# Post norms of a decoder layer: weights and squares taken by channel at copy-out, sums of squares on GpSimd and TensorE

## The reference

```python
def rmsnorm(x, g):
    return x * rsqrt(mean(x * x, axis=-1, keepdims=True) + 1e-6) * g

x = x + rmsnorm(merged @ w_out, g_mix_post)                    # token mixing: SSM branch + sparse attention branch
c = rmsnorm(x, g_x_pre)
x = x + rmsnorm(cross_attention(c, mem_kv, w_xq, w_xo), g_x_post)
m = rmsnorm(x, g_mlp_pre)
hid = square(relu(m @ w_up))
x = x + rmsnorm(hid @ w_down, g_mlp_post)
```

## Time and profile before

| | |
|---|---|
| median of three runs | 1191.24 us |
| profiled execution, span | 1194.3 us (no other time of it is recorded) |
| TensorE matmul busy | 1136.4 us, 95% |
| VectorE busy | 635.8 us, 53% |
| ScalarE busy | 461.8 us, 39% |
| GpSimd busy | 166.1 us, 14% |
| mean granted clock of TensorE | 0.987 |
| share of TensorE in the chain that ended last | 77% |

### The profile page before, as it was taken

The page is one execution under the profiler, slowest core; times in us unless marked ns, Lnnn a source line. Parts: engine busy times, 40 slices in busy tenths (PEclk is TensorE's granted clock), DMA queues, the critical chain, the costliest instruction groups (busy, mean ns, idle before and its releaser), DMA issues.

```text
span 1194.3 us, 21756 instructions
## 1 busy us (share of the span) xinstructions
PE 1136.4 (95%) x8378; PEld 1011.1 (85%) x8378; DVE 635.8 (53%) x1143; ACT 461.8 (39%) x755; POOL 166.1 (14%) x281
## 2 busy tenths in 40 slices
PE   6999999999999998999999988999999999999997
PEld 5888787778777676788897987899999989999997
DVE  4467992765665524311537566546543345666663
ACT  3100320455775414200234475454332334545540
POOL 1020024735302222000000020001000000001100
PEclk9999999998999999999999999999999999999998
DMA  7792254734719448454565626742443223232201
GB/s 199 167 230 63 81 181 141 189 108 123 175 51 291 142 142 283 129 166 128 151 190 182 209 72 195 251 141 85 142 142 106 71 76 101 72 106 71 71 1 75
DMA packets 167105, 164.21 MB, mean 137 GB/s; under 512 B 41573, under 2 KB 148034, under 8 KB 166874
## 3 DMA queue, kind: packets, MB, share of 16 engines
q1 hardware_dynamic: 157658, 134.84, 37.7%
q0 software_dynamic: 9344, 27.98, 7.9%
HBM read 154.21 MB, written 12.73 MB: 140 GB/s over the span
## 4 chain that ended last, share of the span: by engine, by line
PE 77%; SPq 7%; DVE 5%; issue 4%; ACT 4%; DMA 1%; POOL 1%; DVEq 0%; ACTq 0%
PE banks L1485 22%; PE banks L1004 15%; PE banks L1740 15%; PE banks L1439 4%; PE banks L1222 3%; SPq L667 2%; PE banks L1421 2%; SPq L647 2%; PE banks L1010 2%; SPq L696 1%; PE banks L1334 1%; DVE rounded L2818 1%; PE banks L1274 1%; PE banks L1285 1%; PE banks L1257 1%
## 5 line engine op out<-in xcount | busy, mean ns | idle before, releaser
L1485 PE MATMUL banks<-rounded 128*128 128x288 f32 (+1 forms) x2304 | 297.4, 289 | 1.4 <-DVE rounded L2864 0.9
L1485 PEld LDWEIGHTS banks<-rounded 128*128 128x128 f32 x2304 | 292.0, 189 | 4.8 <-issue 2.9
L1004 PE MATMUL banks<-arena 128*128 128x256 f32 x960 | 223.9, 393 | 2.3 <-issue 1.8
L1004 PEld LDWEIGHTS banks<-arena 128*128 128x128 f32 x960 | 181.0, 190 | 38.8 <-issue 1.9
L1740 PE MATMUL banks<-rounded 128*128 128x272 f32 x1536 | 195.1, 290 | 3.8 <-DVE rounded L3046 3.8
L1740 PEld LDWEIGHTS banks<-rounded 128*128 128x128 f32 x1536 | 194.5, 190 | 4.5 <-issue 3.1
L2818 DVE TENSOR_TENSOR rounded<-arena,rounded 128x2048 fp32r<-128x2048 f32 x54 | 125.5, 2324 | 65.5 <-ACT rounded L1963 65.4
L3046 DVE TENSOR_TENSOR rounded<-arena,rounded 128x1088 fp32r<-128x1088 f32 x64 | 82.9, 1304 | 60.2 <-ACT rounded L2207 60.2
L1963 ACT ACTIVATE rounded<-arena 128x2048 fp32r<-128x2048 f32 x54 | 102.9, 1906 | 4.1 <-DMA arena<-in_w_out 4.1
L2207 ACT ACTIVATE rounded<-arena 128x1088 fp32r<-128x1088 f32 x64 | 71.1, 1114 | 81.0 <-PE banks L1740 79.8
L2048 ACT ACTIVATE arena<-banks 128x256 f32<-128x256 f32 (+1 forms) x64 | 25.4, 397 | 126.4 <-PE banks L1485 126.4
(11 more groups left out here) (432 smaller groups left out, 1416.5 us busy)
## 6 DMA issues: line engine op xcount, KB each, us to landing
arena<-in_w_up SPq DMA_DIRECT2D x22, 1024.0 KB, 5.6
arena<-in_w_down SPq DMA_DIRECT2D x16, 1024.0 KB, 5.1
arena<-in_w_in SPq DMA_DIRECT2D x13, 1024.0 KB, 8.8
upper<-in_cache_nsa_kv SPq DMA_DIRECT2D x64, 128.0 KB, 2.4
upper<-in_cache_nsa_kv POOLq DMA_DIRECT2D x64, 128.0 KB, 4.7
arena<-in_w_out SPq DMA_DIRECT2D x8, 1024.0 KB, 5.6
arena<-in_cache_mem_kv SPq DMA_DIRECT2D x16, 512.0 KB, 8.1
arena<-in_cache_nsa_kv SPq DMA_DIRECT2D x90, 64.0 KB, 2.3
```

What stands on the lines that cost most here:

```text
L1004: ins = mm(bank(b + h, (NA, NB)[h], rows=M), lhsT(k), rhs[:, k, toks], start=(k == 0), stop=(k == K - 1))
L1485: ins = mm(bank(b, N), w[:, k], a[:, k, toks], start=(k == 0 and z == 0), stop=(k == K - 1 and z == 2))
```

## The change

The squares and the gain of the first two post norms move ahead of the transposes, where the data lie by channel.

- `y_take` now does two ScalarE passes over each unit's bank: a square into `nsq` (two slots in turn), and the copy into `yTA` or `yTB`, with the channel's gain as scale. The gains are loaded by channel into `gnorm` (16 columns) in place of the two rows `gP` and `gP2`.
- GpSimd adds the squares up over the eight units (`square_sums`, six additions for each half and layer into `nsum`; the last square stays separate). ScalarE's square m, from the third on, waits until GpSimd has done sum m-1; the first two wait for the scaling of the half before.
- TensorE multiplies `nsum` and the last square by a column of ones, token tile by token tile (`norm_sums`, matmuls of one column, four for half A and six for half B), which gives the sums by token. They take a turn of the two banks (`("NS", q)` in `late`).
- VectorE scales these (`sums_scale`), GpSimd raises them to -1/2, two token tiles in one call (and one more call for the sample tile in half B).
- `post` is one VectorE pass: transposed tile times root plus x. `y_square` is gone.
- The order of all engines in this part is written anew.

The core of the diff:

```diff
-            sp.dma_start(gP[:, :], A["g_mix_post"][0].partition_broadcast(P)).then_inc(sem("gP_in"), 16)
+            for i, n in enumerate(("g_mix_post", "g_x_post")):
+                sp.dma_start(gnorm[:, i * 8:i * 8 + 8], A[n][0].rearrange("(k p) -> p k", p=P),
+                             allow_slow_non_contiguous=True).then_inc(sem("gP_in"), 16)
...
+            def square_sums(q, first=1, last=7):
+
+                for m in range(first, last):
+                    u = q * 8 + m
+                    w = half_of("AB"[q % 2])[1]
+                    pool.wait_ge(sem("norm_squares"), u + 1)
+                    if m > 1:
+                        pool.wait_ge(sem("norm_sums"), q * 6 + m - 1)
+                    pool.tensor_tensor(nsum[:, 0:w], nsq[:, 0, 0:w] if m == 1 else nsum[:, 0:w], nsq[:, m % 2, 0:w], ALU.add)\
+                        .then_inc(sem("norm_sums"), 1)
...
+            def norm_sums(q):
+
+                b = late_bank(("NS", q), sem("sums_scaled"), q + 1)
+                pe.wait_ge(*step("ones_set"))
+                pe.wait_ge(sem("norm_sums"), q * 6 + 6)
+                pe.wait_ge(sem("norm_squares"), q * 8 + 8)
+                for i, t in enumerate(HALVES[q]):
+                    n, at = tile_rows(t), tok0(t) - tok0(HALVES[q][0])
+                    for j, part in enumerate((nsum, nsq[:, 1])):
+                        ins = mm(bank(b, 1, i, rows=n), part[:, at:at + n], ones, start=(j == 0), stop=(j == 1))
+                signal(ins, "late_mm")
...
                 act.wait_ge(sem("late_mm"), late_at[name] + 1)
-                signal(fn((yTA if half == "A" else yTB)[:, m, :], bank(late_at[name] % 2, N), ACT.Copy), "proj_out")
+                if m >= 2:
+                    act.wait_ge(sem("norm_sums"), q * 6 + m - 1)
+                elif q:
+                    act.wait_ge(sem("sums_scaled"), q)
+                signal(fn(nsq[:, m % 2, 0:N], bank(late_at[name] % 2, N), ACT.Square), "norm_squares")
+                if q == 0 and m == 0:
+                    act.wait_ge(sem("gP_in"), 32)
+                signal(fn((yTA if half == "A" else yTB)[:, m, :], bank(late_at[name] % 2, N), ACT.Copy,
+                          scale=gnorm[:, i * 8 + m:i * 8 + m + 1]), "proj_out")
...
-                link(stt(ps, ps, r, (gP, gP2)[i][0:n, :], ALU.mult, ALU.mult))
-                signal(tt(x[0:n, t, :], x[0:n, t, :], ps, ALU.add), "x_new")
+                dve.wait_ge(sem("post_T"), NT * i + TILES.index(t) + 1)
+                signal(stt(x[0:n, t, :], ps, r, x[0:n, t, :], ALU.mult, ALU.add), "x_new")
```

More of the change, by code:

```diff
@@ L946, in _, with inverse_rms @@
                 sel_pages(pool, gg, 3, known)
-            def inverse_rms(n):
-                for _ in range(n):
-                    e = rms_n[0]
-                    rms_n[0] += 1
-                    n_rows = TS if squares[e][1] == 4 else P
+            def inverse_rms(first, last):
+                for at in range(first, last):
+                    kind, t = roots[at]
+                    if kind == "NS":
+                        pool.wait_ge(sem("sums_scaled"), t + 1)
+                        parts = sum_columns(t)
+                        for n, c, w in parts:
+                            ins = pool.tensor_tensor(rstd2[0:n, c:c + w], var2[0:n, c:c + w], mhalf[0:n].to_broadcast([n, w]), ALU.pow)
+                            ins.then_inc(sem("inverse_rms"), 1)
+                        continue
+                    e = square_at[kind, t]
+                    n_rows = TS if t == 4 else P
                     pool.wait_ge(sem("squares"), e + 1)
@@ L970, in _, with root @@
             signal(pool.memset(qz, 0.0), "qz_zeroed")
-            inverse_rms(20)
+            def root(kind, t):
+                inverse_rms(root_at[kind, t], root_at[kind, t] + 1)
+            square_sums(0)
+            root("NS", 0)
+            root("x0", 0)
+            root("x0", 1)
+            square_sums(1)
+            root("NS", 1)
+            square_sums(2, 1, 2)
+            root("x0", 4)
+            square_sums(2, 2, 3)
+            root("x0", 2)
+            square_sums(2, 3, 5)
+            root("x0", 3)
+            square_sums(2, 5, 7)
+            root("NS", 2)
+            root("x1", 0)
+            root("x1", 1)
+            square_sums(3)
+            inverse_rms(root_at["NS", 3], len(roots))
             for m in range(3):
-                pool.wait_ge(sem("squares"), SQ0 + 4 * m + 4)
+                pool.wait_ge(sem("squares"), SQN + 4 * m + 4)
                 for j in range(2):
@@ L2767, in inverse_rms, with sums_scale @@
             def inverse_rms(kind, t):
-                e = square_at[(kind, t)]
-                dve.wait_ge(sem("inverse_rms"), e + 1)
-                return rstd2[0:P if kind == "mem" else tile_rows(t), e:e + 1]
+                if kind[0] == "y":
+                    q = 2 * int(kind[1]) + (t >= 2)
+                    e, at = y_col[kind, t], roots_done["NS", q]
+                else:
+                    e, at = square_at[kind, t], roots_done[kind, t]
+                dve.wait_ge(sem("inverse_rms"), at)
+                return rstd2[0:P if kind == "mem" else tile_rows(t), e:e + 1]
+            def sums_scale(q):
+                v = late_at["NS", q]
+                dve.wait_ge(sem("late_mm"), v + 1)
+                for n, c, w in sum_columns(q):
+                    ins = ts(var2[0:n, c:c + w], bank(v % 2, w, 0 if n == P else 2, rows=n), 1.0 / D, EPS, ALU.mult, ALU.add)
+                    if q % 2 and n == P:
+                        own(ins)
+                signal(ins, "sums_scaled")
             for t in range(2):
@@ L3011, in _ @@
             hid_square(8)
+            sums_scale(3)
             post(1, 4)
```

143 lines of the change are left out of this document (72 added, 71 removed).

## The result

The changed kernel takes 1196.86 us (median of 15 runs, 1192.87 to 1199.63), the kernel before 1191.24 us in the runs beside it. The ratio, estimated from all runs of the two, is 1.0034, 95% interval 1.0022 to 1.0046: slower by 4.1 us (the two medians are 5.6 us apart). That is inside what I had called no change (0.5%), but on the other side from the forecast of 1189.5 us, and the median lies just above the range. The profiled execution took 1198.49 us, with a span of 1196.5 us against 1194.3 us.

A forecast was written before the change was run, and what follows sets the result against it. TensorE, busy 1136.4 of 1194.3 us, was taken as the bound, with about 12 us to win. Terms 0.1 + 0 + 2.2 + 0 - 0.7 gave 1.6 to 1.7 us: 1191.24 - 1.7 = 1189.5 us, range 1183.8 to 1196.5.

The forecast's parts named there:

- the clock term: B half's query projection was to start at full clock, gaining 0.7 us; no half clock was costed behind the new waits.
- the wait before xoA1: New 2.7 us TensorE wait before the A half's second cross-projection unit, since ScalarE's first take awaits the scaled sums.
- Rival (d): Clock falls again at the query projection and the new wait: 0.7 us not gained, 0.7 lost, 1190.9 us; chance 0.12.
- the first wait: TensorE waits 3.1 us before the A half's second pre transpose; its low part stands behind a split and two passes.
- 615 to 646: Trace stretch in us up to the A half's query projection; early norm given back at a wait, gain 0.1 us.
- 646 to 692: Trace stretch in us with the output projection; square, sum and copy fit even behind a split, change 0.
- 692 to 722: Trace stretch in us up to the B half's query projection: 1.5 us earlier start plus 0.7 of clock, together 2.2.
- 782 to 830: Trace stretch in us with the B half's last cross-projection units: late take and sums outweigh gains, net loss 0.7 us.
- the loop: ScalarE's square and GpSimd's sum wait on each other; 1.2 us a turn, 1.3 for 288 columns, barely fitting the cross projection.
- (c): The removed pass was hidden anyway and the one-column products, 3.5 us, are simply added: 1194.7 us; chance 0.16.
- (b): Slower: the ScalarE-GpSimd loop sets the cross projection's pace, costing 7.5 us: 1197 us; chance 0.15.
- (a): The chains really get shorter: waits and loop holdups do not form, 7.8 us gained, 1183.4 us; chance 0.19.

## Why the prediction was wrong

**What failed** is the clock term. The prediction let the wait before xoA1 form, put the clock behind it at 1.00 and even counted 0.7 us of clock gained at the query projection; the argument was that the new idle pieces are shorter than the old one. The gain at the query projection came (the first two units take 6.66 us instead of 7.22). But behind the new waits the clock was 0.50, which cost 1.2 us on average at the first (1.7 in the profile shown: 29.57 against 27.89) and 2.4 us at the second. Rival (d) had this mechanism at one new wait, sized 0.7 us; with both places at their measured sizes it gives 1189.5 + 1.2 + 2.4 = 1193.1. By the ratio the changed kernel is at 1195.3; the other 2 us are the smaller errors below (0.2, 0.4 and 0.6 us) and what the interval of 1.4 us to either side leaves open. Rival (d) had a chance of 0.12 and should have had more: the earlier trace rows showed that one-column products with a wait beside them run at half, and both stand ahead of xoA1. I compared idle pieces by length and did not ask what TensorE did around them. For the first wait, with full branch units ahead of it, no row of before told: a piece of 3.3 us had half clock behind it, pieces of 2.9 us together had not the earlier trace rows.

**615 to 646.** The wait was forecast 18.9 us into the stretch and of 3.1 us; it came after 19.1 us and was 3.0 us. The stretch was to gain 0.1 us (the prediction's own terms give 0.2: 637.15 + 0.87 + 4 x 1.94 is 645.8, not 645.9) and lost 1.5, all of it the half clock. With the wait filled the stretch is 30.63 us, 0.2 under the 30.80 of before. The step is right in its mechanism and lacks the clock.

**646 to 692.** 0 forecast, +0.2 measured. Sums beside a split took 1.9 us here, and nothing waited for them on TensorE.

**692 to 722.** 1.5 us of gain was forecast; without the clock the profile would have 1.1 of it (30.46 - 2.4 = 28.1, against 29.24). Right but for the clock and 0.4 us.

**782 to 830.** Forecast: 2.0 us lost to the loop at the last units, 1.0 for the sums, 2.3 back, net 0.7; measured net 1.3. The loop cost 1.8 (with it relaxed the stretch is 42.5), the group of products 1.16, so 1.7 came back. This is the other, smaller error, 0.6 us.

**Prices.** Sums 0.74 and 0.81 us: measured 0.73 and 0.80. A sum inside a split waits for its rest: 2.61 us measured. One turn of the loop with 288 columns took 1.37 us where nothing met it (squares at 798.60 and 799.97), 1.3 forecast. The fused pass 1.28 us as the multiply was. One-column products 3.5 us in all: 0.95 + 1.16 + 0.97 + 1.16 = 4.2 by busy time, and 4.4 us, clock and all, when doubled; so (c) was no rival as to their price alone.

**Rivals.** (b) ended nearest, 1197, but for the wrong reason: the loop gives back 3.0 us when relaxed by itself, 7.5 were forecast, and TensorE's largest waits have nothing to do with it. (a), 1183.4, is what the change gives once the three things are mended: 1183.44 with the orders and the loop changed. That the figures agree is luck: (a) let the first wait, the loop's cost in the B half and 1 us before the query projection vanish; it had no term for the wait before xoA1 or for the clock, and moving the scaling alone took 3.6 us off that stretch (29.04 to 25.42). The gain was there; the written order and one semaphore count gave it away.

## What to carry to other kernels

Where a change puts narrow products in front of a wait on TensorE, cost the piece as a whole: its length, and then a stretch at half clock, which lasted 3.4 or 6.8 us in these profiles and cost 1.5 to 3 us each. Look in the trace for pieces of that kind, narrow work included, not for idle time alone. If the wait can't be moved, wide matmuls into a free bank can pay for themselves: ten of 256 columns gained as much here as 21 did (3.5 and 2.4 us, not told apart). And a producer that waits for its reader should wait for the last reader of that buffer only: one turn of slack was worth 3 us here.

## What the runs showed of the hardware

TensorE's granted clock fell from 2.4 to 1.2 GHz while it was issuing without a gap, in a piece of 13 one-column products (4.05 us), and again, with the products doubled, in one of 12 such products (2.36 us) and the transposes behind them. Each was seen in one profile. It did not fall behind 1.42 us of idle after ten wide matmuls, nor behind 1.33 us between units of 288 columns. The Trainium skill, TensorE: Matmul & The Clock Gate, section "What's actually happening", says that the default state is the throttled one and that activity releases it. The runs agree as far as they go: with ten wide matmuls ahead of an idle piece the clock stayed up (1.00), in a piece full of one-column products it did not (0.50).

The same wait of 3.0 us cost the full clock in five profiles of eight, with the same instructions right ahead of it. A single profile does not price such a place; several do.

The Trainium skill, SBUF — State Buffer, section "SBUF: two separate sides", describes the lock between GpSimd and VectorE that the prediction weighed. The trace of the changed kernel agrees: a 0.80 us sum that starts 0.34 us into a split of 2.29 us ends 0.66 us after it, whereas in the other order, a split that meets a running sum of 544 columns, VectorE was the one held up, 3.20 us. The prediction also took from that section that the fused pass, which reads PSUM, would not be in a sum's way, and had no trace of it. The changed kernel's timeline has one, and it agrees: a sum that runs inside a fused pass, neither of them longer than alone.

```profile
709.46 1.28 DVE L2920 SCALAR_TENSOR_TENSOR arena<-banks,arena 128x1024 f32<-128x1024 f32 x1 [3.40 <-PE banks L1574]
...
709.60 0.75 POOL L987 TENSOR_TENSOR arena<-arena 128x256 f32<-128x256 f32 x1 [0.56 <-ACT arena L2056]
```
